# A transposed product moved into the next level of a triangular inverse, and the order of the copies behind it

## The reference

```
def rwkv7_bidir_scan(r, w, k, v, a, b):
    ...
    def step(state, inp):
        r_t, w_t, k_t, v_t, a_t, b_t = inp
        sa = jnp.einsum('dbhij,dbhj->dbhi', state, a_t)
        state = (state * w_t[..., None, :] + sa[..., :, None] * b_t[..., None, :]
                 + v_t[..., :, None] * k_t[..., None, :])
        y = jnp.einsum('dbhij,dbhj->dbhi', state, r_t)
        return state, y
```

## Time and profile before

| | us |
|---|---|
| median of 3 runs | 1623.55 |
| lowest, highest | 1619.76, 1632.7 |
| the profiled execution's own time | 1613.03 |
| its span, first to last instruction | 1611.1 |
| mean granted clock of TensorE in it | 0.992 |

### The profile page before, as it was taken

The page is one execution under the profiler, slowest core; times in us unless marked ns, Lnnn a source line. Parts: engine busy times, 40 slices in busy tenths (PEclk is TensorE's granted clock), DMA queues, the critical chain, the costliest instruction groups (busy, mean ns, idle before and its releaser), DMA issues.

```text
span 1611.1 us, 35745 instructions
## 1 busy us (share of the span) xinstructions
PE 1540.1 (96%) x15477; PEld 1479.2 (92%) x15477; DVE 1065.5 (66%) x1285; ACT 732.5 (45%) x814; POOL 69.6 (4%) x51
## 2 busy tenths in 40 slices
PE   7999999998999999999998999999988899999998
PEld 7999999887999999999988999999866778999997
DVE  5776487764766547765577776476767775877446
ACT  5443345542534335333455433364564434455333
POOL 2000000100100001000101000021000000100000
PEclk9999999999999999999999999999999999999999
DMA  8565545201555556655533665554300012565552
GB/s 273 183 198 193 191 150 174 89 2 54 182 184 182 184 185 186 200 187 201 179 119 105 186 201 187 196 190 158 127 31 3 3 55 77 172 195 185 198 195 79
DMA packets 155064, 243.25 MB, mean 151 GB/s; under 512 B 9283, under 2 KB 106174, under 8 KB 154814
## 3 DMA queue, kind: packets, MB, share of 16 engines
q1 hardware_dynamic: 154510, 240.63, 45.8%
q10 hardware_dynamic: 432, 0.79, 0.2%
HBM read 240.34 MB, written 1.05 MB: 150 GB/s over the span
## 4 chain that ended last, share of the span: by engine, by line
PE 87%; DVE 8%; ACT 3%; issue 2%; DMA 1%; POOL 0%; SPq 0%; ACTq 0%; DVEq 0%
PE dense_ps L2495 24%; PE dense_ps L2496 24%; PE dense_ps L2497 24%; PE mixer_ps L450 1%; DVE w_lo L2865 1%; PE mixer_ps L538 1%; PE dense_ps L450 1%; PE mixer_ps L1755 1%; PE mixer_ps L1183 1%; PE mixer_ps L1174 0%; DVE xT L2983 0%; DVE x_raw L622 0%; DMA raw<-in_ffn_w_gu 0%; ACT score_b L1213 0%; ACT w_hi L2692 0%
## 5 line engine op out<-in xcount | busy, mean ns | idle before, releaser
L2865 DVE TENSOR_TENSOR w_lo<-raw,w_hi 128x2048 fp32r<-128x2048 f32 x225 | 523.1, 2336 | 240.6 <-ACT w_hi L2692 239.7
L2495 PE MATMUL dense_ps<-h_hi,w_hi 128*128 128x256 f32 x2368 | 665.1, 281 | 11.7 <-DVE h_lo L2940 8.1
L2497 PE MATMUL dense_ps<-h_hi,w_lo 128*128 128x256 f32 x2368 | 658.9, 278 | 0.0
L2496 PE MATMUL dense_ps<-h_lo,w_hi 128*128 128x256 f32 x2368 | 658.9, 278 | 0.0
L2692 ACT ACTIVATE w_hi<-raw 128x2048 fp32r<-128x2048 f32 x225 | 428.7, 1914 | 330.9 <-DMA raw<-in_ffn_w_down 115.1
L2495 PEld LDWEIGHTS dense_ps<-h_hi,w_hi 128*128 128x128 f32 x2368 | 448.7, 189 | 17.8 <-issue 17.3
L2496 PEld LDWEIGHTS dense_ps<-h_lo,w_hi 128*128 128x128 f32 x2368 | 446.7, 189 | 0.8 <-issue 0.5
L2497 PEld LDWEIGHTS dense_ps<-h_hi,w_lo 128*128 128x128 f32 x2368 | 446.7, 189 | 0.0
L2495 PE MATMUL dense_ps<-g_hi,w_hi 128*128 128x256 f32 x960 | 265.8, 277 | 0.0
L2496 PE MATMUL dense_ps<-g_lo,w_hi 128*128 128x256 f32 x960 | 265.8, 277 | 0.0
L2497 PE MATMUL dense_ps<-g_hi,w_lo 128*128 128x256 f32 x960 | 265.8, 277 | 0.0
(11 more groups left out here) (553 smaller groups left out, 1777.0 us busy)
## 6 DMA issues: line engine op xcount, KB each, us to landing
raw<-in_ffn_w_gu SPq DMA_DIRECT2D x176, 512.0 KB, 4.7
raw<-in_ffn_w_down SPq DMA_DIRECT2D x88, 512.0 KB, 4.0
raw<-in_w_ff SPq DMA_DIRECT2D x64, 512.0 KB, 4.2
raw<-in_w_in SPq DMA_DIRECT2D x36, 512.0 KB, 4.3
raw<-in_a_w_in SPq DMA_DIRECT2D x32, 512.0 KB, 4.4
raw<-in_a_w_out SPq DMA_DIRECT2D x8, 512.0 KB, 4.1
raw<-in_b_w_in SPq DMA_DIRECT2D x8, 512.0 KB, 4.1
raw<-in_b_w_out SPq DMA_DIRECT2D x8, 512.0 KB, 4.1
```

What stands on the lines that cost most here:

```text
L2495: pe.matmul(o, hi, mh, start=start, stop=False)
L2496: pe.matmul(o, hi, ml, start=False, stop=False)
L2497: return pe.matmul(o, lo, mh, start=False, stop=stop)
L2865: dve.tensor_tensor(w_lo[:, p % SLOTS, :], raw[:, p % SLOTS, :], w_hi[:, p % SLOTS, :].bitcast(F32), ALU.subtract).then_inc(lo_ready, 1)
```

## The change

TensorE: the transposed product of half 0 no longer stands directly behind Z of half 0 but behind Z of half 1; that of half 1 is issued only in the next level, between that level's Y of half 0 and Y of half 1 (ahead of the wait for x of half 1). Level 6 keeps its form. VectorE: in every level both x are merged first, half 0 and half 1, and then both xt. The bodies of the copies are the same, written as two functions.

```
+        def transposed(half):
+            quads(pe, D_ps[:, half, :], half, lambda s_: y[:, s_, :], lambda s_: xt[:, s_, :]).then_inc(zt_mm, 1)
...
                 else:
+                    if lv > 1 and half == 1:
+                        transposed(1)
                     pe.wait_ge(x_up, 12 * batch + 2 * (lv - 1) + half + 1)
...
                 if lv < LEVELS - 1:
                     crossed(pe, half, lambda s_: xt[:, s_, :], lambda s_: y[:, s_, :]).then_inc(z_mm, 1)
-                    quads(pe, D_ps[:, half, :], half, lambda s_: y[:, s_, :],
-                          lambda s_: xt[:, s_, :]).then_inc(zt_mm, 1)
...
+            if lv < LEVELS - 1:
+                transposed(0)
```

```
+        def plain(lv, half):
+            to, data = x[:, 4 * half:4 * half + 4, :], bank_pair(half)
+            if lv == 0:
+                dve.wait_ge(y_mm, 14 * batch + half + 1)
+            else:
+                dve.wait_ge(z_mm, 12 * batch + 2 * (lv - 1) + half + 1)
+            alone(dve)
...
+        def turned_(lv, half):
+            to, data = xt[:, 4 * half:4 * half + 4, :], banks(half, 1, D_ps)
+            if lv:
+                dve.wait_ge(zt_mm, 12 * (batch - GROUPS_A) + 2 * (lv - 1) + half + 1)
...
+            end_.then_inc(inv_up, 1)
         for lv in range(LEVELS):
             for half in range(2):
-                if lv == 0:
-                    dve.wait_ge(y_mm, 14 * batch + half + 1)
...
+                plain(lv, half)
+            for half in range(2):
+                turned_(lv, half)
             beside(lv)
```

More of the change, by code:

```diff
@@ L598, in inverse4_dve @@
     def inverse4_dve(dve, nt_of, x, xt, batch, beside):
+        def plain(lv, half):
[5 more added lines that the diff above has]
+            alone(dve)
+            if lv == LEVELS - 1:
+                a, b = NEED_R[0]
+                dve.tensor_copy(to[64:P, a:b, 0:64], data[64:P, a:b, 0:64])
+            else:
+                dve.copy_predicated(out=blocks(to, lv, 0), mask=merge_mask("merge", lv),
+                                    data=blocks(data, lv, 0)).then_inc(x_up, 1)
@@ new lines, in turned_ @@
+        def turned_(lv, half):
+            to, data = xt[:, 4 * half:4 * half + 4, :], banks(half, 1, D_ps)
+            if lv:
+                dve.wait_ge(zt_mm, 12 * (batch - GROUPS_A) + 2 * (lv - 1) + half + 1)
+            if lv == LEVELS - 1:
+                a, b = NEED_R[1]
+                end_ = dve.tensor_copy(to[0:64, a:b, 64:P], data[0:64, a:b, 64:P])
+            elif lv == 0:
+                mask_ = merge_mask("merge_t", lv)[:, 0:2]
+                dve.copy_predicated(out=blocks(to[:, 0:2], lv, 1), mask=mask_, data=blocks(nt_of(half), lv, 1))
+                end_ = dve.copy_predicated(out=blocks(to[:, 2:4], lv, 1), mask=mask_, data=blocks(data[:, 2:4], lv, 1))
+            else:
+                end_ = dve.copy_predicated(out=blocks(to, lv, 1), mask=merge_mask("merge_t", lv),
+                                           data=blocks(data, lv, 1))
+            end_.then_inc(inv_up, 1)
@@ L626, in inverse4_dve @@
-                end_.then_inc(inv_up, 1)
+                plain(lv, half)
+            for half in range(2):
+                turned_(lv, half)
             beside(lv)
```

## The result

| | before | after |
|---|---|---|
| median, 20 runs each (us) | 1618.96 | 1632.78 |
| lowest, highest | 1610.77, 1632.7 | 1621.2, 1639.85 |
| the profiled execution | 1613.03 | 1629.38 |
| mean granted clock in it | 0.992 | 0.986 |

What follows compares the result with a forecast made beforehand. TensorE bounds the kernel; in the inverses the order of waits decides. Tile 0's 0.75 plus 2 x 0.82 minus tile 3's 0.94 gives +1.45 us: 1614.5 profiled, 1625.0 median, range 1613 to 1634.

Steps and rivals of the forecast that it cites:

- the likeliest case: Whole kernel: waits add 1.45 us, 1612.7 to 1615.3 us on the profiled execution's footing; chance 0.55.
- the clock falls: Rival: longer TensorE gap brings the lower clock behind tiles 0 and 2 too; +4.9 us, 1628.4; chance 0.15.
- (a): TensorE, levels where it is late: next level's half 1 product loads at 1.79 us against 1.84; steady level gains 0.05.
- (b): VectorE, tiles 0 to 2: xt1 waits for its queued transposed product; x0 of level 6 1.02 us late in tile 1.
- my lower bound: Sum at least -0.3 us; includes -0.6 if the level 6 product's half issues in 0.24 us for 0.43.
- VectorE's idle time before xt1: Sign in the inverse: VectorE idles about 0.45 us before xt1 in level 4 and 0.65 in level 5.
- (c): VectorE's last four copies in level 6: two of three steps stay on one partition side, -0.20 us per tile.
- (d): Tile 3's inverse, without key work: TensorE's gains reach the end, so apply's first product comes 0.94 us earlier.
- My price: Clock rival's cost: two more falls, behind tiles 0 and 2, 1.7 us for a fall, 3.4 us added.
- xt1's idle sum: Sign on VectorE: xt1's group, with no idle time before, gets 4 to 8 us.
- the copies' steps: Sign at the inverse's end: VectorE's last copies step 0.21, 0.31, 0.21 us.
- the gap before L1773: Sign before apply: TensorE's gap grows from 1.29 to about 2.1 us in tiles 0 to 2.

Runs made afterwards that it cites:

- after twice: The full change against the kernel before, measured in two separate runs: ratio 1.006, then 1.005.
- TensorE's part: Kernel before with only the changed TensorE order of products, VectorE's copies in the old order: ratio 1.0055 against the kernel before.
- the longer gap: Kernel before plus one unused VectorE reduction in tiles 0 to 2, lengthening TensorE's idle time before apply: ratio 0.998 against the kernel before.
- the later load: Changed kernel with the feed-forward weights' load begun one ScalarE step later: ratio 1.0004 against the kernel before.
- VectorE's part: Kernel before with only VectorE's new copy order, TensorE's program as before: ratio 1.0002 against the kernel before.
- own level: Changed kernel with half 1's transposed product back at the end of its own level, VectorE's new order kept: ratio 0.9989 against the kernel before.
- levels 1 to 3: Change in levels 1 to 3 only, levels 4 and 5 as before, new order of level 6's last copies: ratio 1.0021 against the kernel before.

## Why the prediction was right and wrong

**The sign and the size.** I forecast +1.45 us, 1.0009; measured is 1.006. The time, 1632.8, is inside the range, but the likeliest case was not what happened: the waits came at about their forecast sum, and on top of them the rival "the clock falls", which I gave 0.15 and 3.4 us.

**(a) TensorE's steady level** held. Y0 loads 0.48 behind x0's start (I had 0.51), T1 at once behind it, Y1 1.85 behind Z0 (I had 1.79 with an x0 that started 0.09 sooner), which is what before has, 1.84.

**(b) The new wait** was right in mechanism and place, too large in size. T1's load to xt1's start is 0.73 in level 4 and 0.80 in level 5 (I took 0.75). Tile 1, step by step: x0 of level 4 is 0.26 earlier (I said 0.10); from there to x0 of level 5 takes 3.04 us against 2.62, +0.42 (I said 0.45); xt1 in level 5 starts S+1.47 against S+1.01, +0.46 (I said 0.67). The last is the term that was mis-sized: I let the level 6 product L564 hold T1 for 0.43 us, and it held it 0.18 (1270.56 to 1270.74), less than the 0.24 of my lower bound. Its half is four products, where a half of L538 is eight (x8 against x16 in the rows). The 0.65 us of the earlier trace rows from which I had it were too long for another reason: there the last products of T1 were still being issued between those of L564.

```profile
1261.08 0.28 PE L450 MATMUL dense_ps<-xt_r,ly_r 64*64 64x64 f32 x3
...
1261.15 0.27 PE L450 MATMUL dense_ps<-xt_r,ly_r 64*64 64x64 f32 x2
```

VectorE's idle time before xt1 was 0.35 and 0.36, not 0.45 and 0.65; the two groups have 5.4 us idle (I said 4 to 8).

**(c) The last copies**: 1273.30 to 1274.22 is 0.92 against 1.14 before, -0.22 where I had -0.20. The held start at a change of partitions is what the Trainium skill (VectorE: DVE Perf Modes, Two Vector instructions with no wait between them) has, and this trace agrees. Tile 1 together: -0.26+0.42+0.46-0.22=+0.40, measured +0.41; forecast +0.82.

**(d) Tile 3** failed in the profile: +0.25 for -0.94. Z0 of level 1 came 0.46 earlier (I had 0.5) and x0 of level 2 0.75, and then the 0.88 us stand behind the weights' burst took it. Where the burst is moved, Z0 of level 3 comes 0.93 earlier and that of level 5 1.21 (I had 1.06 and 1.37), and tile 3 is 18.24: -1.03 against before. So the working on the engines' order was right in the main. What I had put at nothing was the supply of TensorE's instructions: a transfer of some 400 GB/s in the same stretch makes them late, and the sooner TensorE arrives, the longer it stands. The sum of the inverses, +1.29 for +1.45, is thus right by luck: tiles 1 and 2 at half their size, the gain of (d) missing.

**The clock.** My price had two more falls, of 1.7 us each. In the profiled execution there were three more, and those of tile 0 and tile 3 cost 2.7 and 2.8: +7.1. Over all runs, the mean clock fell from 0.987 to 0.984, and 0.0029 of 1612 us are 4.7 us, an estimate; with the waits' 1.3 that makes 6.0 of the 9.7 us measured (interval 6.3 to 13.1), so a part of some 0.3 us or more, 3.7 by the middle, is not accounted for. The mean clock is a blunt measure of this stage: reckoned in the same way, the profiled executions lose 8 to 17 us ahead of it, where nothing was changed. That the changed kernel comes back to before once the products hold the clock is shown; why the clock fell more often is not. Behind gaps of 1.48 to 1.64 us (after twice, TensorE's part, the longer gap, the later load) 14 of 15 applies of tiles 0 to 2 fell, behind 1.05 to 1.29 (before, VectorE's part, own level, levels 1 to 3) 5 of 12, and with products in the gap 0 of 15. Against it stand the longer gap's twelve runs, and tile 3, where a gap of 1.02 or 1.03 was followed by a fall in four executions and by none in three, one of 0.83 by a fall (TensorE's part) and one of 0.96 twice by none. The Trainium skill (TensorE: Matmul & The Clock Gate, Part 1) says that idleness throttles and that the point varies between runs. That it varies is seen here; that the idle time by itself decides is not.

**What I had said would show it**: VectorE's idle time before xt1 came (smaller), xt1's idle sum came, the copies' steps came (0.21, 0.30, 0.21); the gap before L1773 is 1.54, not 2.1, the inverse of tile 1 +0.4, not +0.8; tile 3 missed. Before has one fall in its profiled execution, at a mean clock of 0.992 where its runs have 0.987: I built on an execution luckier than most.

## What to carry to other kernels

An operation moved behind an instruction that waits inherits that wait, and so does all that is queued behind its reader: put it at the end of its own step, where its operands are ready, and reorder the reader's queue to match (19.5 us an inverse, against 20.2 before and 20.6). In a stretch of small products with pauses, look at the granted clock of the dense part behind it before counting tenths of a microsecond, and over many executions; a few spare products in a pause that can't be removed held it there, and lengthened the inverses of tiles 0 to 2 by 0.05 us at most where the clock was level. Their wait and cost have to be looked at each time: in tile 3 the inverse of before went from 19.27 to 20.16, 0.77 us of it a stand for instructions. Before trusting a sum over engines, look at what the DMA engines do in the same stretch, and at when the packets of the instruction queue land.

## What the runs showed of the hardware that I had not expected

With products in the pause before it, an apply was never at the lower clock (0 of 15 in tiles 0 to 2; mean clock 0.989 to 0.992), and four such products are enough. The lower clock can still come elsewhere: in one of these kernels the inverse of tile 0 had 0.92. Behind a pause of one length the fall comes in one execution and not in the next.

In the inverse of tile 3 TensorE stood between two of its own weight loads for 0.67 to 1.44 us, with no releaser named, in nine of the twelve executions with the feed-forward weights' load at its old place; not in before, in TensorE's part alone and in the longer gap. In seven of the nine the stand began after the last packet of the feed-forward weights, in two in the midst of them (some 370 and 420 GB/s). What the stands have in common is the instruction queue: each ends 1.3 to 1.5 us behind the landing of one of its 16 KB packets, which came late beside the weights' load. It is a stretch of many short instructions: a half's 16 issue in some 0.24 us. In the two executions where the load came later there is no stand over 0.33 us, nor is there one in tile 1's inverse of before.
